# Head sums of the first head pair as products on half of TensorE's array

## The reference

```
p = (h @ w_qkv).reshape(b, t, N_GROUPS, 3, H_SLOT, HEAD_DIM)
q = rmsnorm(p[:, :, :, 0], q_norm)      # over the 64 elements of each head
k = rmsnorm(p[:, :, :, 1], k_norm)
rmsnorm(x, g) = x * rsqrt(mean(x * x, axis=-1) + EPS) * g
```

## Time and profile before

| | us |
|---|---|
| median of three runs (lowest, highest) | 1442.25 (1439.96, 1442.99) |
| the profiled execution, its own time | 1439.33 |
| its span in the profile | 1437.8 |
| TensorE matmuls busy (PE) | 1397.2 (97%) |
| TensorE weight loads busy (PEld) | 1351.2 (94%) |
| VectorE (DVE) busy | 772.9 (54%) |
| ScalarE (ACT) busy | 500.5 (35%) |

### The profile page before, as it was taken

One profiled execution on the slowest core, in us unless ns is written; L12 is line 12 of the kernel. 1 busy time (PEld: TensorE's weight loads), 2 busy tenths in 40 slices (PEclk: granted clock), 3 DMA queues, 4 the chain that ended last, 5 costly groups with the idle time before them and its releaser, 6 DMA issues.

```text
span 1437.8 us, 27814 instructions
## 1 busy us (share of the span) xinstructions
PE 1397.2 (97%) x11152; PEld 1351.2 (94%) x11152; DVE 772.9 (54%) x1255; ACT 500.5 (35%) x801; POOL 21.1 (1%) x50
## 2 busy tenths in 40 slices
PE   5999999999999999999999999989899999999998
PEld 4999999999999999999899899877799999999998
DVE  5655565565655433445655646647575656553223
ACT  3322234334333332334334333323353343332210
POOL 0000000000000000000000000000000000000000
PEclk9999999999999999999999999998799999999999
DMA  6344436653544444547526317247224454445331
GB/s 168 89 147 147 147 107 188 189 165 102 165 131 152 139 135 132 160 124 217 151 68 208 109 57 217 87 121 184 88 74 134 134 170 117 132 156 159 108 93 60
DMA packets 254953, 195.16 MB, mean 136 GB/s; under 512 B 6485, under 2 KB 248645, under 8 KB 253730
## 3 DMA queue, kind: packets, MB, share of 16 engines
q1 hardware_dynamic: 251304, 137.04, 34.0%
q0 software_dynamic: 1792, 54.43, 10.6%
q10 hardware_dynamic: 1786, 2.67, 0.5%
HBM read 186.60 MB, written 65.21 MB: 175 GB/s over the span
## 4 chain that ended last, share of the span: by engine, by line
PE 92%; DVE 4%; ACT 1%; issue 1%; DMA 1%; ACTq 0%; SPq 0%; DVEq 0%
PE acc L1436 78%; PE N L1425 3%; PE M L1604 2%; PE acc L1703 2%; PE N L1636 2%; PE acc L1464 1%; PE M L1628 1%; PE M L1624 1%; DMA skv<-new_rows 1%; DVE wl L973 0%; DMA big<-in_x_sample_dram 0%; PE M L1606 0%; PE M L1605 0%; ACT hh L704 0%; PE M L1464 0%
## 5 line engine op out<-in xcount | busy, mean ns | idle before, releaser
L1436 PE MATMUL acc<-hh,wh 128*128 128x260 f32 x2288 | 468.3, 286 | 2.2 <-DVE wl L973 2.2
L1436 PE MATMUL acc<-hh,wl 128*128 128x260 f32 x2288 | 462.8, 284 | 0.0
L1436 PE MATMUL acc<-hl,wh 128*128 128x260 f32 x2288 | 462.3, 284 | 0.0
L687 ACT ACTIVATE wh<-wraw 128x1024 fp32r<-128x1024 f32 (+1 forms) x212 | 220.7, 1041 | 549.1 <-PE acc L1436 540.8
L1436 PEld LDWEIGHTS acc<-hh,wh 128*128 128x128 f32 x2288 | 356.3, 190 | 4.3 <-issue 2.4
L1436 PEld LDWEIGHTS acc<-hh,wl 128*128 128x128 f32 x2288 | 354.9, 190 | 0.0
L1436 PEld LDWEIGHTS acc<-hl,wh 128*128 128x128 f32 x2288 | 354.4, 189 | 0.0
L973 DVE TENSOR_TENSOR wl<-wraw,wh 128x1024 fp32r<-128x1024 f32 (+1 forms) x212 | 254.3, 1200 | 174.0 <-ACT wh L687 168.6
L1436 PE MATMUL acc<-yh,wh 128*128 128x260 f32 x848 | 173.1, 285 | 0.0
L1436 PE MATMUL acc<-yh,wl 128*128 128x260 f32 x848 | 171.8, 284 | 0.0
L1436 PE MATMUL acc<-yl,wh 128*128 128x260 f32 x848 | 171.3, 284 | 0.0
(11 more groups left out here) (192 smaller groups left out, 1192.0 us busy)
## 6 DMA issues: line engine op xcount, KB each, us to landing
out_dram<-in_cache_kv_d_dram POOLq DMA_DIRECT2D x24, 1364.0 KB, 6.3
wraw<-in_ffn_w_gate_dram SPq DMA_DIRECT2D x44, 512.0 KB, 3.8
wraw<-in_ffn_w_up_dram SPq DMA_DIRECT2D x44, 512.0 KB, 3.9
wraw<-in_attn_w_qkv_dram SPq DMA_DIRECT2D x36, 512.0 KB, 4.0
out_dram<-in_cache_kv_d_dram POOLq DMA_DIRECT2D x8, 2044.0 KB, 8.3
wraw<-in_ffn_w_down_dram SPq DMA_DIRECT2D x32, 448.0 KB, 3.8
wraw<-in_sc_w_in_dram SPq DMA_DIRECT2D x24, 512.0 KB, 3.8
wraw<-in_ffn_w_down_dram SPq DMA_DIRECT2D x16, 512.0 KB, 3.9
```

Of the source, the lines that this page charges most:

```text
L687: nc.scalar.activation(wh[c % 2][:, 0:k], wraw[:, c % 4, 0:k], ACT.Copy).then_inc(hi_done, 1)
L1436: ins = T.matmul(acc[:, par, h2, 0:HALF], w[c % 2][:, k, :], a[:, k0 + k, h2, :], start=(first and k == 0 and n == 0), stop=(last and k == ...
```

## The change

For the six head sums of pair 0 alone (q = 0 to 5) the full product with `head_ones` is replaced. An even q works in tiles of 64 rows: the squares of head 0 (partitions 0 to 63, `lo`) and head 1 (`hi`) are multiplied separately and added up in `N`. First `lo` goes to the first half of the positions and `hi` to the second, then, after a new semaphore has said that these are complete, `hi` to the first and `lo` to the second. An odd q works in tiles of 64 columns: for each half of the positions one product fills partitions 0 to 63 of `N` and one partitions 64 to 127. The other 18 head sums stay.

```diff
@@ -272,6 +272,7 @@
         qk_ready = sem("qk_ready")
         qsq_ready = sem("qsq_ready")
         qms_ready = sem("qms_ready")
+        half_sums = sem("half_sums")
         inv_ready = sem("inv_ready")
         norm_ready = sem("norm_ready")
         s_ready = sem("s_ready")
@@ -1632,8 +1633,22 @@
             def head_sums(q):
 
                 pe.wait_ge(qsq_ready, q + 1)
-                for h2 in range(2):
-                    ins = T.matmul(N[:, h2, 0:HALF], head_ones[:], sq[:, h2, :], start=True, stop=True)
+                lo, hi = slice(0, DH), slice(DH, P)
+                if q < 6 and q % 2 == 0:
+                    for i, (a, b) in enumerate(((lo, hi), (hi, lo))):
+                        if i:
+                            ins.then_inc(half_sums, 1)
+                            pe.wait_ge(half_sums, q // 2 + 1)
+                        for h2, s in enumerate((a, b)):
+                            ins = T.matmul(N[:, h2, 0:HALF], head_ones[s, :], sq[s, h2, :], start=(i == 0),
+                                           stop=(i == 1))
+                elif q < 6:
+                    for h2 in range(2):
+                        for s in (lo, hi):
+                            ins = T.matmul(N[s, h2, 0:HALF], head_ones[:, s], sq[:, h2, :], start=True, stop=True)
+                else:
+                    for h2 in range(2):
+                        ins = T.matmul(N[:, h2, 0:HALF], head_ones[:], sq[:, h2, :], start=True, stop=True)
                 ins.then_inc(qms_ready, 1)
 
             def n_read(p, c):
```

## The result

The changed kernel takes 1443.18 us (median of 18 runs, 1441.44 to 1446.23), the kernel before 1439.04 on the same chips (median of 18, 1436.19 to 1442.99). The ratio is 1.0030, with a 95% interval of 1.0023 to 1.0038: 4.3 us slower, between 3.3 and 5.5. The forecast difference, +4.9 us, lies in that. The forecast time, 1447.2, and its range, which began at 1444.0, do not hold 1443.18.

A forecast was written before the change was run, and what follows sets the result against it. TensorE was taken to bound the kernel, its matmuls busy 97% of the span. Three row sums (+3.2) and three column sums (+1.7) gave +4.9 us on the median 1442.25: 1447.2, range 1445.2 to 1448.6, 8 in 10 1444.0 to 1450.9.

The forecast's parts named there:

- What bounds the kernel: Whole kernel and pair 0: TensorE's matmuls busy 97% of the span, so a head sum's TensorE time is paid in full.
- A pass in a half tile still takes u: Head sums of pair 0: a 260-column pass on half the array still takes 0.22 us, the whole array's distance between passes.
- Pipelined pairs: Two-tile products in pair 0: three pass times per pair, 1.32 us by rows, 1.10 by columns; chance 0.45.
- B1 can run beside A2: Two passes each on tiles A and B: B's first overlaps only A's second, so three pass times of 0.22 us, not four.
- My third case: Rival for the six sums: both tiles fully side by side, two pass times per pair, +2.9 us, 1445.2; chance 0.18.
- the sign of both tiles side by side: Timeline of a sum by columns: first to last start takes 0.66 us or less if both tiles run together.
- Changes of form: Around pair 0's half-array sums: 0.18 us to go in by rows, 0.14 by columns, 0.20 to come back.
- The wait: Inside each sum by rows: TensorE waits for its own pass, 0.16 tail, 0.04 start, 0.11 uncovered load, 0.31 us together.
- The clock: Rival at q = 0: half-array sums let the clock fall to 0.50, 1.5 us more, +6.4 in all, 1448.7; chance 0.08.
- The signs that I had named for being wrong: Pair 0: chunk to chunk grows by under 0.2 or over 1.6 us, or the clock leaves 1.00 between 607 and 665.
- Sum: Six head sums of pair 0: three by rows +3.2 us, three by columns +1.7, in all +4.9 us.
- The absolute time: Whole kernel: +4.9 us added to the runs' median 1442.25, not to the profiled execution's 1439.33, giving 1447.2 us.

The follow-up runs named there:

- the order experiment: The changed kernel with the four products of a sum by columns issued tile A, A, B, B instead of A, B, A, B: 1444.35 us, ratio 1.0024.

## Why the prediction was wrong, point by point

**What bounds the kernel:** right. All that a head sum in pair 0 took longer came out in full; VectorE and ScalarE were busy for 772.9 and 500.4 us as before, and the matmul records rose to 11176 as forecast. One reading was off without effect: by the earlier trace rows the chain behind a head sum ends 2.2 us after the sum's end, and 3.2 after its start.

**A pass in a half tile still takes u:** right, 0.22 us in every form.

**Pipelined pairs:** wrong, and this is the step of the mechanism that failed. I wrote that "B1 can run beside A2", since passes start in order of issue. The runs show A1 and B1 starting within 0.01 us, B's ahead of three later passes of A that were issued before it. A pair takes 2 u, not 3, and four products in columns 4 u, not 5. That made the forecast 3 x 0.44 + 3 x 0.22 = 2.0 us too dear. My third case had it, at 0.18, and its terms (0.69 and 0.34) were measured as 0.72 and 0.35. The Trainium skill, TensorE: Matmul & The Clock Gate, The mechanism, has different tiles start some 4 ns apart; the trace agrees, with 0.01 us. From a column sum's first start to its last it took 0.7 us, near the 0.66 that I had named as the sign of both tiles side by side and far from 0.88. I had set this aside because of the order of passes, for which I had no row. The same section holds that matmuls are in strict order of issue; for two tiles the order experiment contradicts it, and the measurement decides.

**Changes of form:** right. 0.14 into columns was 0.15, 0.18 into rows showed as 0.64 - 0.44 = 0.20 in the sum without a wait, the way back 0.19 to 0.20. One of my rows was misread: the products of line 1628, from which a head sum came back with 1.07, use the form of 64 columns and not of 64 rows. The price was the same.

**The wait:** 0.31 forecast, 0.33 measured, twice. But I priced only its own time. At q = 0 it comes on top of the idle 1.56 us, and there the clock fell.

**The clock:** held to be a rival of 0.08, and blamed on half the array. It came and cost the 1.5 us that I had put on it, by luck: I had 3 us at half the pace, it was 3.4 us at 0.55 of the pace. And it came for another reason: the same fall comes with full products and a wait, and with full products behind a longer idle time, and not with half-array sums that follow at once. I had put the kernel's evidence, idle 1.56 us and clock at 1.00, down as safety; 0.33 us of waiting more, or 0.68 of idle time more, was enough. The signs that I had named for being wrong were both there: the clock left 1.00, and from the first head sum to the second it took 8.97 us instead of 6.91, 2.1 more and not at most 1.6.

**Sum:** 4.9 - 2.0 + 1.5 = 4.4 us, against 4.5 on the chain and 4.3 by the runs. The forecast of the difference was right through two errors that cancelled. It must not be read as a success of its steps.

**The absolute time:** wrong, and this step put the measured time outside the range. The step was "I add the sum to the median". That median, 1442.25, was of three runs; 18 of the same kernel gave 1439.04. The profiled execution, 1439.33, was nearer, and with it the same sum gives 1444.2 (measured 1443.18). I treated the 2.9 us between them as spread of the profile, not of the median, and let my range reach down only 3.2 us from the forecast, while the before-runs alone spread over 3. (The bounds of the forecast's own range are 0.1 to 0.2 us too wide by its own terms, which changes nothing.)

## What to carry to other kernels

Half-array products of different tiles run side by side, so they lost nothing and won nothing here, where a pass is bound by its 260 columns; what they cost is the change of form, 0.35 us a visit, so they belong beside other work of the same form. They pay where the weight load is the bound: there two tiles load at once. And a wait that TensorE makes for itself next to an idle stretch must be priced with the clock, not by its length alone.

## What the runs showed of the hardware that was not expected

- TensorE starts the passes of one tile ahead of passes of another tile issued earlier, but not far ahead: with 24 passes of tile A issued first, 20 went by before tile B began, beside the 21st.
- Weight loads of two 64-column tiles run at the same time: 48 pairs of loads and 2-column passes in 2.90 us, 0.06 each, against 0.12 for one load of 128 columns.
- The wait of TensorE for its own result, between two products, costs 0.33 us in the form of 64 rows and on the full array alike.
